# Retention layer of a two-layer encoder trunk: chunks of 128 tokens instead of 256 in the recurrent core

## What is computed

```python
def retention_layer(h, w_in, w_out):            # h: normed, 4 heads, q/k width 256, v width 512
    q, k, v, g = jnp.split(h @ w_in, ...)
    q = apply_rope(q); k = apply_rope(k) * RET_QK_DIM ** -0.5
    sc = jnp.einsum('bnhid,bnhjd->bnhij', qc, kc) * decay_in      # inside a chunk, causal
    o_inner = jnp.einsum('bnhij,bnhje->bnhie', sc, vc)
    def step(R, inp):                                             # from chunk to chunk
        o = jnp.einsum('bhid,bhde->bhie', q_i, R) * xi
        R_new = g_chunk * R + jnp.einsum('bhjd,bhje->bhde', k_i * zeta, v_i)
        return R_new, o
    o = o_inner + o_cross                                         # then a norm over each head's 512 values
    y = o * jax.nn.silu(g)
    return y @ w_out
```

## Time and profile before

| | |
|---|---|
| median of 3 runs | 2501.65 us (2501.47 to 2503.18) |
| the profiled execution's own time | 2501.99 us |
| its span, first to last instruction | 2500.0 us |
| mean granted TensorE clock | 0.998 of full speed |
| PE busy | 2457.7 us of the span (98%) |
| DVE, ACT, POOL busy | 1145.1, 568.8, 137.5 us |
| matmuls | 11600 |

### The profile page before, as it was taken

One profiled execution on the slowest core, in us unless ns is written; L12 is line 12 of the kernel. 1 busy time (PEld: TensorE's weight loads), 2 busy tenths in 40 slices (PEclk: granted clock), 3 DMA queues, 4 the chain that ended last, 5 costly groups with the idle time before them and its releaser, 6 DMA issues.

```text
span 2500.0 us, 29536 instructions
## 1 busy us (share of the span) xinstructions
PE 2457.7 (98%) x11600; PEld 2039.9 (82%) x11600; DVE 1145.1 (46%) x1999; ACT 568.8 (23%) x1314; POOL 137.5 (6%) x145
## 2 busy tenths in 40 slices
PE   7999999999999999999999999999999999999998
PEld 6888888877888888888888888888788888888877
DVE  6454554578533233336642423333764233333384
ACT  2221211234211121223411102112441121212142
POOL 2111112211000000000000000000000000000000
PEclk9999999999999999999999999999999999999999
DMA  8766665645644434343554343534255434354433
GB/s 354 271 239 266 241 257 207 252 162 223 236 169 167 168 134 176 130 169 115 208 218 181 137 172 131 201 133 169 92 229 219 158 148 181 134 184 153 168 99 146
DMA packets 43834, 462.41 MB, mean 185 GB/s; under 512 B 4832, under 2 KB 5472, under 8 KB 14560
## 3 DMA queue, kind: packets, MB, share of 16 engines
q1 hardware_dynamic: 34864, 425.07, 45.5%
q10 hardware_dynamic: 8880, 36.18, 3.9%
HBM read 358.47 MB, written 102.76 MB: 184 GB/s over the span
## 4 chain that ended last, share of the span: by engine, by line
PE 91%; DVE 6%; issue 1%; ACT 1%; DMA 0%; POOL 0%; DVEq 0%; SPq 0%; ACTq 0%; POOLq 0%
PE ps L456 29%; PE ps L458 29%; PE ps L457 29%; DVE fr L1030 1%; PE ps L710 1%; PE ps L584 1%; DVE ff L1306 1%; DVE mx L1346 1%; PE ps L720 1%; PE ps L521 1%; DVE ff L1377 0%; DMA raw<-in_stream 0%; DVE whl L1075 0%; ACT ff L981 0%; DVE xlo L1030 0%
## 5 line engine op out<-in xcount | busy, mean ns | idle before, releaser
L456 PE MATMUL ps<-whl,xhi 128*128 128x512 f32 (+1 forms) x1408 | 543.3, 386 | 0.8 <-DVE xlo L1030 0.5
L458 PE MATMUL ps<-whl,xlo 128*128 128x512 f32 (+1 forms) x1408 | 535.9, 381 | 0.0
L457 PE MATMUL ps<-whl,xhi 128*128 128x512 f32 (+1 forms) x1408 | 534.4, 380 | 0.0
L456 PE MATMUL ps<-xhi,whl 128*128 128x512 f32 x768 | 304.7, 397 | 16.6 <-DVE xlo L1034 16.5
L458 PEld LDWEIGHTS ps<-whl,xlo 128*128 128x128 f32 x1408 | 264.8, 188 | 51.7
L456 PE MATMUL ps<-whl,fr 128*128 128x512 f32 x768 | 305.7, 398 | 0.0
L456 PEld LDWEIGHTS ps<-whl,xhi 128*128 128x128 f32 x1408 | 265.2, 188 | 48.7 <-issue 0.9
L457 PEld LDWEIGHTS ps<-whl,xhi 128*128 128x128 f32 x1408 | 265.4, 188 | 47.8
L458 PE MATMUL ps<-whl,fr 128*128 128x512 f32 x768 | 301.2, 392 | 0.0
L458 PE MATMUL ps<-xhi,whl 128*128 128x512 f32 x768 | 300.3, 391 | 0.0
L457 PE MATMUL ps<-xlo,whl 128*128 128x512 f32 x768 | 300.2, 391 | 0.0
(11 more groups left out here) (135 smaller groups left out, 2637.2 us busy)
## 6 DMA issues: line engine op xcount, KB each, us to landing
whl<-split_w SPq DMA_DIRECT2D x132, 2048.0 KB, 7.8
split_w<-whl SPq DMA_DIRECT2D x44, 2048.0 KB, 7.3
raw<-in_stream SPq DMA_DIRECT2D x44, 1024.0 KB, 9.4
ff<-in_x_t ACTq DMA_DIRECT2D x8, 1024.0 KB, 9.8
hres<-in_x ACTq DMA_DIRECT2D x4, 2048.0 KB, 9.2
out<-hres ACTq DMA_DIRECT2D x16, 512.0 KB, 5.4
ff<-in_x ACTq DMA_DIRECT2D x3, 2048.0 KB, 15.0
whl<-split_w SPq DMA_DIRECT2D x6, 1024.0 KB, 6.5
```

The lines of the kernel that those rows point to most:

```text
L456: pe.matmul(dst, lhs[0], rhs[0], start=start, stop=False)
L457: pe.matmul(dst, lhs[0], rhs[1], start=False, stop=False)
L458: return pe.matmul(dst, lhs[1], rhs[0], start=False, stop=stop)
```

## The change

The core's chunks become 128 tokens, the size of a tile, so a block has four of them. Scores shrink to the four diagonal 128x128 squares of a head, all in bank 4, masked by one DVE operation, copied by one ACT operation, with the remainder by one DVE operation (two or four of each before). `update(c)` is 6 matmuls instead of 12, into banks 0,1 for even c and 2,3 for odd c, and there are four (three in block 3). `cross(t)` has a wait of its own for `r_lo`. `inner(t)` is always 3 matmuls. State update, `r_hi` and `r_lo` happen once for each chunk. `cross(3)` is issued after the first tile of the gate projection, behind `inner(3)`, and now closes bank 7. Two small DVE operations before the power become one.

PE's order is now: `update(0)`; wait for v_lo 4; `update(1)`; `cross(0)` (not in block 0); `inner(0)`; `update(2)`; `cross(1)`; `inner(1)`; `update(3)` (not in block 3); `cross(2)`; `inner(2)`; `inner(3)`; gate tile 0; `cross(3)`; gate tile 1 and on.

The diff, cut to its core (buffers, the constant `decay_of` for `col(12)`, and ACT's same copies are left out):

```diff
@@ -44,8 +44,7 @@
 HEADS, DK, DV = 4, 256, 512
-RC = 256
-SEEN = RC + P
+RC = 128
 SH, SKV, SD = 16, 2, 64
@@ -155,7 +153,7 @@
         khl = [fr[:, 2048 + i * 1024:2048 + (i + 1) * 1024].rearrange("p (d t) -> p d t", d=2) for i in range(2)]
-        shl = [fr[:, 2048 + i * 1024:2048 + (i + 1) * 1024].rearrange("p (c m) -> p c m", c=2)[:, :, 0:SEEN] for i in range(2)]
+        shl = [fr[:, 2048 + i * 1024:2048 + i * 1024 + BT] for i in range(2)]
         kthl = [fr[:, 4096 + i * 1024:4096 + (i + 1) * 1024].rearrange("p (t d) -> p t d", t=TT) for i in range(2)]
@@ -170,7 +168,7 @@
         krot = ff[:, 4096:5120].rearrange("p (d t) -> p d t", d=2)
-        smask = ff[:, 5120:6144].rearrange("p (c m) -> p c m", c=2)[:, :, 0:SEEN]
+        smask = ff[:, 5120:5120 + BT]
         qt = ff[:, 0:4096].rearrange("p (i n f c) -> p i n f c", i=2, n=NCH, f=4)
@@ -233,19 +231,18 @@
         kt_lo = count("kt_lo", head=1)
-        s_mm = count("scores", head=2)
-        s_masked = count("scores_masked", head=4)
-        s_hi = count("s_hi", head=2)
-        s_lo = count("s_lo", head=2)
-        u_mm = count("state_update", head=2)
-        a_new = count("state_new", head=2, credit=1)
-        r_hi = count("r_hi", head=2)
-        r_lo = count("r_lo", head=2)
-        o_cross = count("o_cross_terms", head=1)
+        s_mm = count("scores", head=1)
+        s_masked = count("scores_masked", head=1)
+        s_hi = count("s_hi", head=1)
+        s_lo = count("s_lo", head=1)
+        u_mm = count("state_update", head=4)
+        a_new = count("state_new", head=4, credit=1)
+        r_hi = count("r_hi", head=4)
+        r_lo = count("r_lo", head=4)
+        o_cross = count("o_cross_terms", head=3)
         o_mm = count("o_tile", head=4, credit=1)
...
         o_mv = count("o_mean_var", head=4)
-        o_var1 = count("o_var_scaled", head=1)
         o_var = count("o_var", head=1)
@@ -524,13 +521,11 @@
                     pe.wait_ge(k_lo.sem, at(k_lo, 1))
-                    for c in range(2):
-                        for k in range(2):
-                            for d in range(2):
-                                key, qry = slice((2 * c + k) * P, (2 * c + k + 1) * P), slice(c * RC + k * P, (c + 1) * RC)
-                                mm = three(ps[:, 4 + c, k * RC:RC + k * P], [v[:, d, key] for v in khl],
-                                           [v[:, d, qry] for v in qhl], d == 0, d == 1)
-                        mm.then_inc(s_mm.sem, 1)
+                    for c in range(TT):
+                        tok = slice(c * RC, (c + 1) * RC)
+                        for d in range(2):
+                            mm = three(ps[:, 4, tok], [v[:, d, tok] for v in khl], [v[:, d, tok] for v in qhl], d == 0, d == 1)
+                    mm.then_inc(s_mm.sem, 1)
@@ -539,45 +534,46 @@
                         for d in range(2):
-                            for k in range(2):
-                                t = 2 * c + k
-                                mm = three(ps[:, 2 * c + d, :], [v[:, t, d * P:(d + 1) * P] for v in kthl],
-                                           [v[:, t, :] for v in vhl], k == 0, k == 1)
+                            mm = three(ps[:, 2 * (c % 2) + d, :], [v[:, c, d * P:(d + 1) * P] for v in kthl],
+                                       [v[:, c, :] for v in vhl], True, True)
                             if first and c == 0 and d == 0:
...
-                    def cross(t):
+                    def cross(t, begin=True):
+                        pe.wait_ge(r_lo.sem, at(r_lo, t + 1))
                         for d in range(2):
                             mm = three(ps[:, 4 + t, :], [v[:, d, t * P:(t + 1) * P] for v in qhl],
-                                       [v[:, d, :] for v in rhl], d == 0, False)
-                        return mm
-
-                    def inner(t, alone=False):
-                        c = t // 2
-                        for k in range(t % 2 + 1):
-                            mm = three(ps[:, 4 + t, :], [v[:, c, (t % 2 + k) * P:(t % 2 + k + 1) * P] for v in shl],
-                                       [v[:, 2 * c + k, :] for v in vhl], alone and k == 0, k == t % 2)
-                        mm.then_inc(o_mm.sem, 1)
+                                       [v[:, d, :] for v in rhl], begin and d == 0, not begin and d == 1)
+                        mm.then_inc(o_cross.sem if t < 3 else o_mm.sem, 1)
+
+                    def inner(t, begin=False):
+                        mm = three(ps[:, 4 + t, :], [v[:, t * P:(t + 1) * P] for v in shl],
+                                   [v[:, t, :] for v in vhl], begin, t < 3)
+                        if t < 3:
+                            mm.then_inc(o_mm.sem, 1)
...
                     pe.wait_ge(v_lo.sem, at(v_lo, 2))
-                    update(0, 2 if last else 1)
-                    pe.wait_ge(r_lo.sem, at(r_lo, 1))
-                    pe.wait_ge(s_lo.sem, at(s_lo, 2))
+                    update(0)
+                    pe.wait_ge(v_lo.sem, at(v_lo, 4))
+                    update(1)
+                    pe.wait_ge(s_lo.sem, at(s_lo, 1))
                     if not first:
                         cross(0)
-                        cross(1).then_inc(o_cross.sem, 1)
                     inner(0, first)
-                    inner(1, first)
-                    pe.wait_ge(v_lo.sem, at(v_lo, 4))
+                    pe.wait_ge(a_new.sem, at(a_new, 1))
+                    update(2, 2 if last else 1)
+                    cross(1)
+                    inner(1)
                     if not last:
-                        update(1)
-                    pe.wait_ge(r_lo.sem, at(r_lo, 2))
-                    for t in (2, 3):
-                        cross(t)
-                        inner(t)
+                        pe.wait_ge(a_new.sem, at(a_new, 2))
+                        update(3)
+                    cross(2)
+                    inner(2)
+                    inner(3, True)
+
@@ -589,8 +585,10 @@
                             if c == 4 and t % 2 == 0:
-                                pe.wait_ge(a_new.sem, at(a_new, t // 2 + 1))
+                                pe.wait_ge(a_new.sem, at(a_new, t // 2 + 3))
                             mm = over_tokens(t, t, c, DV, xs, 4 * (c - 4), 4, c == 4, c == 5)
+                            if c == 4 and t == 0:
+                                cross(3, False)
                             if c == 5 and t < 3:
@@ -892,10 +889,11 @@
                         act.activation(vhl[0][:, t, :], ps[:, t, :], ACT.Copy, scale=vcol[:, h, t:t + 1]).then_inc(v_hi.sem, 1)
-                    act.wait_ge(a_new.sem, at(a_new, 1))
-                    act.wait_ge(o_cross.sem, at(o_cross, 1))
-                    act.sem_inc(passed, 1)
-                    act.activation(rhl[0].rearrange("p d e -> p (d e)"), st, ACT.Copy, scale=col(12)).then_inc(r_hi.sem, 1)
+                    for c in range(1, TT):
+                        act.wait_ge(a_new.sem, at(a_new, c))
+                        act.wait_ge(o_cross.sem, at(o_cross, c))
+                        act.sem_inc(passed, 1)
+                        act.activation(rhl[0].rearrange("p d e -> p (d e)"), st, ACT.Copy, scale=decay_of).then_inc(r_hi.sem, 1)
@@ -1047,7 +1045,7 @@
                 dve.wait_ge(vcol_step.sem, at(vcol_step, 1))
-                dve.tensor_tensor(vcol[:, :, :], rcol[:, :].rearrange("p (h c) -> p h c", h=HEADS)[:, :, 0:4],
+                dve.tensor_tensor(vcol[:, :, :], rcol[:, :].rearrange("p (h c) -> p h c", h=HEADS)[:, :, 0:1].broadcast_to([P, HEADS, 4]),
                                   xrstd[:, :].unsqueeze(1).broadcast_to([P, HEADS, 4]), ALU.mult).then_inc(vcol_done.sem, 1)
@@ -1144,14 +1143,12 @@
                             kthl[0].rearrange("p t d -> p (t d)"), kt_lo)
-                    for c in range(2):
-                        dve.wait_ge(s_mm.sem, at(s_mm, c + 1))
-                        dve.tensor_tensor(smask[:, c, 0:RC], ps[:, 4 + c, 0:RC], tri[:, 0:RC], ALU.mult).then_inc(s_masked.sem, 1)
-                        dve.tensor_tensor(smask[:, c, RC:SEEN], ps[:, 4 + c, RC:SEEN], tri[:, 0:P], ALU.mult).then_inc(s_masked.sem, 1)
-                    for c in range(2):
-                        dve.wait_ge(s_masked.sem, at(s_masked, 2 * c + 2))
-                        dve.wait_ge(s_hi.sem, at(s_hi, c + 1))
-                        less_hi(shl[1][:, c, :], smask[:, c, :], shl[0][:, c, :], s_lo)
+                    dve.wait_ge(s_mm.sem, at(s_mm, 1))
+                    dve.tensor_tensor(smask.rearrange("p (c q) -> p c q", c=TT), ps[:, 4, :].rearrange("p (c q) -> p c q", c=TT),
+                                      tri[:, 0:RC].unsqueeze(1).broadcast_to([P, TT, RC]), ALU.mult).then_inc(s_masked.sem, 1)
+                    dve.wait_ge(s_masked.sem, at(s_masked, 1))
+                    dve.wait_ge(s_hi.sem, at(s_hi, 1))
+                    less_hi(shl[1], smask, shl[0], s_lo)
                     if first:
@@ -1162,8 +1159,14 @@
```

(35 more changed lines are left out.)

4 lines of the change are left out of this document (2 added, 2 removed).

## The result

| | median of the runs, us | lowest to highest | ratio to the kernel before (95%) |
|---|---|---|---|
| before, beside it | 2502.41 | 2501.47 to 2503.29 | |
| after | **2545.49** | 2543.34 to 2547.32 | 1.0172 (1.0154 to 1.0190) |

Slower by 43.1 us, where +32.0 was predicted. The profiled execution took 2543.34 us with a span of 2541.5, against 2501.99 and 2500.0: +41.5 of span is what the trace can divide up. Its mean granted clock is 0.998, as before; it is the fastest of the four, the other three took 2544.24 to 2547.32 us at 0.996 to 0.997.

What follows compares the result with a forecast made beforehand. PE, busy 98%, was taken as the bound. Blocks 1 and 2 +11.6, block 3 +12.6, block 0 +9.4 and scores -1.6 gave +32.0 on 2501.99; less 0.34 for the median, 2533.7 us, range 2523 to 2546.

Steps and rivals of the forecast that it cites:

- Bound and mechanism: Whole kernel: PE, busy 98%, sets the time; in the core, three chained state links per head make it wait.
- Its stalls, one by one: Core, per head: waits at v_lo and before cross terms; net +1.45 us blocks 1 and 2, +3.16 block 3, +2.35 block 0.
- the hop from DVE's end to PE's start: Core, before a stalled matmul: PE starts 0.15 us after DVE finishes, as read from the earlier trace.
- The small stall foreseen there: Block 0, before cross(3): DVE's weight split delays the third remainder to 15.7, a stall of 0.26 us.
- Matmuls removed: Core: six fewer inner matmuls, 1.36 us a head, -10.9 in blocks 1 and 2; narrower scores save 1.6 in all.
- At nothing: End of core, small DVE operation, score masks and copies, load of x: hidden behind other work, costing 0.
- the sum: Whole kernel: block terms 11.6, 12.6 and 9.4 less 1.6 for scores give +32.0 us.
- bounds: Some 48 stalls: each could be 0.2 us shorter (-10) or 0.25 longer (+12); with ends, 2523 to 2546.
- The copy is not held by the cross matmuls: Rival, core: copies follow the state update alone, only the v_lo wait stays; 2497 us, 4%.
- Work alone decides: Rival, core: waits at v_lo 4 and r_lo all covered, block 3 loses its old stall; 2485 us, 4%.
- The clock falls in the core: Rival, core: granted clock drops, losing 1.7 us once in each of 16 heads, +27; 2561 us, 8%.

Runs made afterwards that it cites:

- e3b: Changed kernel with two buffers used in turn for the state's hi/lo copies, against one: 2520.62 us, ratio 1.0071.
- e2: Changed kernel with update(1) and its v_lo wait moved behind cross(0) and inner(0): 2530.47 us, ratio 1.0108.
- e4: Changed kernel with cross(3) put back ahead of inner(3) and the gate projection: 2603.86 us, ratio 1.0406.
- e7: Changed kernel, one buffer, update(1) behind inner(0), and inner(2), inner(3) ahead of update(3) and cross(2): 2513.57 us, ratio 1.0043.
- e1: Changed kernel with the old memory layout restored by 1 KB behind the mask and the dropped column's 16 bytes: 2539.30 us, ratio 1.0145.
- b1: Kernel before with the changed kernel's memory layout (half the mask, small column moved behind the large buffers): 2512.55 us, ratio 1.0039.
- p1: Changed kernel with only the 16 bytes of the dropped column put back, single run: 2540.47 us.
- p2: Changed kernel with only the 1024 bytes behind the mask put back, single run: 2544.73 us.
- e5: Changed kernel with update(1) behind inner(0), two buffers for the state's copies and the old memory layout: 2507.56 us, ratio 1.0019.

## Why the prediction was right in the core and short in the sum

**Bound and mechanism: right.** PE stays the bound, and the core turned from work without a stall to a chain of copy, remainder and cross term. e3b takes the buffer's wait away and the two stalls go; e2 takes v_lo's; e4 takes the cover of `cross(3)` and the fourth stall appears. The forecast's +33.6 for the core was +33.0. PE's waits as the trace counts them are 0.45 (0.5 predicted), 0.67 (0.7 to 0.8) and 2.03 in block 3 (2.1).

**Its stalls, one by one.** Blocks 1 and 2: `update(1)` predicted at T0 + 2.10, measured 2.00; `cross(1)` 7.86 and 7.74; `cross(2)` 12.26 and 12.11; net +1.45 and +1.43, of which 0.05 lies in the gate projection behind `cross(3)`. In each the hop from DVE's end to PE's start was taken as 0.15 from the earlier trace rows and is 0.06 here (925.54 to 925.60), and what that saves comes back in small things: the first matmul after a wait takes 0.33 instead of 0.31, and those that follow stand 0.23 apart, not 0.227. The first head of a block is 0.2 shorter, since there the v_lo wait is 0.26. Block 3: +3.16 predicted, +3.15 measured. Block 0: +2.35 and +2.28. PE's timeline there, head 2 (T0 = 281.64):

```profile
287.32 0.50 PE L453 MATMUL ps<-fr 128*128 128x512 f32 x1 [0.15 <-DVE fr L1032]
...
291.69 0.50 PE L453 MATMUL ps<-fr 128*128 128x512 f32 x1 [0.66 <-DVE fr L1032]
...
297.12 0.39 PE L455 MATMUL ps<-whl,xlo 128*128 128x512 f32 x1
297.41 0.50 PE L453 MATMUL ps<-fr 128*128 128x512 f32 x1
```

`cross(1)` at 5.68, predicted 5.80; `cross(2)` at 10.05, predicted 10.18; `cross(3)` at 15.77, predicted 15.88. The small stall foreseen there exists, though the trace gives it no bracket: the start comes 0.29 after the last one instead of 0.23, right behind the remainder's end at 297.36, and has the 0.50 of a restart.

**Matmuls removed: right.** The 24 narrow score matmuls fill 904.19 to 906.90, 0.113 each; the stage lost 0.08 us a head, 0.1 predicted. The Trainium skill's 81 ns for such a matmul (TensorE: Matmul & The Clock Gate, Back-to-back issue gap) would have made it 1.9 us for 2.7; the measurement disagrees with it again.

**At nothing: right where it named a cover.** Normalizing, the load of x and the copies of scores let nothing through: no wait of PE names them.

**The step that fell short is the sum.** It has terms for stalls and for matmuls added and removed, and puts at nothing, without a reason, those that the diff leaves alone. 1536 matmuls of the output projection each became 0.004 us slower: +6.5, and 768 of layer B's as well: +3.2, while the transposes gain 0.5. All of that hangs on 16 bytes. The remaining 0.6 us of the +3.8 outside the heads is less than single traces can attribute. The stretch between blocks 0 and 1 varies in runs with one address layout: +0.5 in the kernel after, +0.6 in e7 and +4.6 in e2; with the 16 bytes in place +1.9 to +5.4; its mean clock is 0.99 in the short ones and 0.98 in the others. With it varies what a whole run shows of the 16 bytes, as e1's 6.2 and b1's 10 do. The "bounds" only knew hops and restarts, so the range covered this by luck: 2545.5 lies half a microsecond inside its upper end.

**The rivals.** "The copy is not held by the cross matmuls" fell with the copy's release by PE. e3b shows what it would have been, and that the rival was priced too low: core and gate come to +7.8 us there, not its -2.6. Blocks 1 and 2 are as it says (-0.5 a head), but block 3 keeps a wait of 0.8 before `cross(2)`, and block 0 comes to +2.0 a head where it had +0.6. "Work alone decides" needed a v tile remainder by T0 + 1.2; it came at 1.94. "The clock falls in the core" did not happen in the kernel after (clock 0.998), but is closer than 8% makes it seem: block 3 of e2, heads of e4, p1 and p2 all show it, at 1.1 to 1.7 us each, at most the size that the rival gave.

## What to carry to other kernels

Halving a chunk to save matmuls multiplies the links of the recurrence; write down for each link what PE can do meanwhile, and put the work that needs no state (here `inner`) in front of the cross term that waits, with a second buffer so that the copy follows the state and not the reader. Give a change that resizes tensors a control in which only the sizes change: here 16 bytes were worth some 9 us by the pace of the matmuls (the two controls moved by 6 and 10), a fifth of the whole difference, and would have been read as part of the algorithm. Price an idle of some 2 us on PE at up to nearly twice its length (2.0 and 1.7).

## What was not expected of the hardware

- A shift of one operand by 16 bytes made 512-column fp32 matmuls 0.2332 us apart instead of 0.2289, in the output projections of both layers and in both kernels; a shift by 1024 bytes did nothing. In the old kernel the same shift moved the core by 0.6 us in all.
- After one idle of 2.0 us the granted clock fell to 0.57 over 3.7 us in all four heads of block 3 of e2, in three of the eight of p1 and p2, which have the instructions of the kernel after, and in none of the profiled kernel after itself. After idles of 0.7 us it never fell in the core, nor after the 1.57 us in block 3 of e5. The Trainium skill (TensorE: Matmul & The Clock Gate, A second HAM failure mode) tells of idles between groups of matmuls that make the clock swing; three idles of 0.45 to 0.67 us in a core of 16 us did not, in this case's traces.
- PE restarts 0.06 us after DVE's last write here, where 0.15 was read before, and its first matmul takes 0.50 in the trace for 0.39.
